# Hybrid decoder step on one core: VectorE's transposes and copies of a recurrence level put ahead of the serial steps of the pair before

## What is computed

```python
def rwkv_scan(S0, r, w, k, v, kk, a):
    def step(S, inp):
        r_t, w_t, k_t, v_t, kk_t, a_t = inp
        sa = jnp.einsum('bhvk,bhk->bhv', S, kk_t)
        S = S * w_t[:, :, None, :] - sa[..., None] * (kk_t * a_t)[:, :, None, :] + v_t[..., None] * k_t[:, :, None, :]
        y = jnp.einsum('bhvk,bhk->bhv', S, r_t)
        return S, y
    ...
    S, ys = lax.scan(step, S0, xs)
    return S, jnp.swapaxes(ys, 0, 1)
```

## Time and profile before

| | us |
|---|---|
| runs | 1202.17, 1209.87, 1207.2 (median 1207.2) |
| profiled execution | 1205.3 |
| its span, first to last instruction | 1203.5 |
| TensorE busy | 1119.9 (93%) |
| VectorE busy | 464.1 (39%) |
| ScalarE busy | 362.8 (30%) |
| GpSimd busy | 259.9 (22%) |

### The profile page before, as it was taken

One profiled execution on the slowest core, in us unless ns is written; L12 is line 12 of the kernel. 1 busy time (PEld: TensorE's weight loads), 2 busy tenths in 40 slices (PEclk: granted clock), 3 DMA queues, 4 the chain that ended last, 5 costly groups with the idle time before them and its releaser, 6 DMA issues.

```text
span 1203.5 us, 24875 instructions
## 1 busy us (share of the span) xinstructions
PE 1119.9 (93%) x10856; PEld 785.2 (65%) x10856; DVE 464.1 (39%) x930; ACT 362.8 (30%) x808; POOL 259.9 (22%) x153
## 2 busy tenths in 40 slices
PE   6999999999999878787789999989999999999995
PEld 4666666655566657666554444468878887888774
DVE  4200656356765675675744322350101001111024
ACT  4101645344334354564521221211111111011152
POOL 0000000001110169999800000111112112111102
PEclk9999999999999989999999999889999999999998
DMA  6511100010100220002032571169789989999894
GB/s 209 149 36 36 57 19 18 18 35 22 40 22 18 28 44 4 4 4 56 6 127 91 192 267 71 65 208 342 253 303 319 322 297 306 322 326 301 290 389 172
DMA packets 95689, 174.16 MB, mean 145 GB/s; under 512 B 19988, under 2 KB 41175, under 8 KB 95172
## 3 DMA queue, kind: packets, MB, share of 16 engines
q1 hardware_dynamic: 88372, 151.92, 36.5%
q0 software_dynamic: 7200, 20.57, 6.4%
HBM read 147.45 MB, written 27.75 MB: 146 GB/s over the span
## 4 chain that ended last, share of the span: by engine, by line
PE 84%; DVE 9%; ACT 3%; issue 3%; SPq 0%; DMA 0%; POOLq 0%; POOL 0%; DVEq 0%; ACTq 0%
PE ps L740 22%; PE ps L1446 20%; PE ps L1244 9%; PE ps L1469 9%; PE ps L1475 1%; PE ps L819 1%; PE ps L843 1%; PE ps L832 1%; PE ps L956 1%; PE ps L1422 1%; PE ps L944 1%; PE ps L997 1%; DVE ps L2283 1%; DVE arena L2272 1%; PE ps L986 1%
## 5 line engine op out<-in xcount | busy, mean ns | idle before, releaser
L740 PE MATMUL ps<-arena 128*128 128x355 f32 x960 | 298.7, 467 | 1.9 <-issue 1.8
L1446 PEld LDWEIGHTS ps<-arena 128*128 128x128 f32 x2048 | 245.9, 191 | 7.8 <-issue 6.1
L740 PEld LDWEIGHTS ps<-arena 128*128 128x128 f32 x960 | 180.2, 191 | 107.5 <-issue 10.5
L1446 PE MATMUL ps<-arena 128*128 128x128 f32 (+4 forms) x2048 | 248.3, 283 | 0.7 <-ACT arena L1958 0.6
L1244 PE MATMUL ps<-arena 128*128 128x512 f32 x256 | 116.4, 597 | 0.7 <-DVE arena L2346 0.7
L1469 PE MATMUL ps<-arena 128*128 128x512 f32 x256 | 113.3, 595 | 0.7 <-DVE arena L2621 0.7
L1966 ACT ACTIVATE arena<-ps 128x128 f32<-128x128 f32 (+4 forms) x64 | 18.3, 286 | 278.4 <-PE ps L1446 278.4
L2621 DVE TENSOR_TENSOR arena<-arena,ps 128x128 f32<-128x128 f32 (+4 forms) x64 | 19.1, 299 | 212.6 <-ACT arena L1966 212.6
L1469 PEld LDWEIGHTS ps<-arena 128*128 128x128 f32 x256 | 47.4, 190 | 55.1 <-issue 53.6
L2806 POOL TENSOR_TENSOR arena<-arena 128x1024 f32<-128x1024 f32 x4 | 11.4, 2855 | 331.5 <-DVE arena L2147 331.5
L1555 ACT COPY arena<-ps 128x355 f32<-128x355 f32 x60 | 27.2, 453 | 182.5 <-PE ps L740 182.5
(11 more groups left out here) (416 smaller groups left out, 1550.8 us busy)
## 6 DMA issues: line engine op xcount, KB each, us to landing
arena<-in_w_exp_gate SPq DMA_DIRECT2D x16, 2048.0 KB, 10.9
arena<-in_w_exp_up SPq DMA_DIRECT2D x16, 2048.0 KB, 16.0
arena<-in_w_exp_down SPq DMA_DIRECT2D x16, 2048.0 KB, 15.3
arena<-in_w_in SPq DMA_DIRECT2D x16, 512.0 KB, 3.8
arena<-in_x_prompt SPq DMA_DIRECT2D x9, 512.0 KB, 3.7
x_dram<-arena SPq DMA_DIRECT2D x9, 512.0 KB, 3.6
h_dram<-arena SPq DMA_DIRECT2D x8, 512.0 KB, 2.6
out_y_prompt<-arena SPq DMA_DIRECT2D x8, 512.0 KB, 3.5
```

What stands on the lines that cost most here:

```text
L740: last = pe.matmul(ps[:, q % 2, 0:m], wr[:, n % 3, k, :], hT[:, k, a:a + m], start=(k == 0), stop=(k == KB - 1))
L1446: last = pe.matmul(ps[:, 3 + f % 2, n * CAP:n * CAP + CAPS[e]], w[a][:, k, f * P:(f + 1) * P], xgT[:, a, k, 0:CAPS[e]], start=(k == 0), st ...
```

## The change

In the level loop of VectorE's stream, for every pair and level, the calls are written in another order. T1 of the level before stands ahead of `stepped(c)` instead of behind it; the copy of half 0 stands ahead of `stepped(c + 1)`; T0 and the copy of half 1 stand ahead of `stepped(c + 2)`. Nothing else differs.

```diff
--- before.py
+++ after.py
@@ -2405,20 +2405,20 @@
                 r_crossed(hp, 1)
                 for lv in range(1, LV):
                     c = 3 * (lv - 1) + 1
+                    r_transpose(hp, 1, lv - 1)
                     stepped(hp, c)
-                    r_transpose(hp, 1, lv - 1)
                     early_norm(hp, lv)
-                    stepped(hp, c + 1)
                     if lv < LV - 1:
                         r_x_in(hp, 0, lv)
                     else:
                         r_xt_in(hp, 0)
-                    stepped(hp, c + 2)
+                    stepped(hp, c + 1)
                     if lv < LV - 1:
                         r_transpose(hp, 0, lv)
                         r_x_in(hp, 1, lv)
                     else:
                         r_xt_in(hp, 1)
+                    stepped(hp, c + 2)
                     late_norm(hp, lv)
                 if hp >= 2:
                     g_scale(hp - 2, 1, 3)
```

## The result

The changed kernel takes 1197.83 us (median of 15 runs, 1191.21 to 1201.73), the kernel before 1206.09 in the 15 runs beside it (1200.81 to 1211.1). The ratio is 0.9929, 95% interval 0.9912 to 0.9945. By the ratio that is 8.6 us less, between 6.6 and 10.6; the two medians lie 8.3 apart. The profiled execution took 1199.22 us, its span 1197.4, against 1205.3 and 1203.5.

The account below looks back on a forecast made before the run. The last-ending chain is 84% TensorE, so time is won only where TensorE stands still. Terms: 0.8 + 2 x 3.0 = 6.8, less 1.1 for instruction stops, 5.7; 1207.2 - 5.7 = 1201.5 us, range 1195 to 1208.

Parts of the forecast that it names:

- (a): The forecast itself: in the levels, the copy of half 1 stops waiting needlessly; gain 3 to 9.5 us, chance 0.72.
- level 1, each of pairs 2, 3: T1 no longer stands behind `stepped(1)`, and the next T1 comes earlier: 1.25 us gained per pair.
- level 2, each: Pairs 2 and 3: earlier copy of half 1 shortens T1 to T1 from 5.09 to 4.46 us, gain 0.63.
- level 3, each: Pairs 2 and 3: T1 to T1 from 4.49 to 3.84 us, 0.65 on paper, 0.08 taken because of instruction stops.
- level 4, each: Pairs 2 and 3, where gate matmuls wait for `g_scale`: T1 to T1 from 6.47 to 5.73 us, gain 0.74.
- pair 1, to T1 of level 2: TensorE's fills hold the X matmuls as before, but T1 comes at 484.76 against 485.73: 0.97 us gained.
- level 5, each of pairs 2, 3: TensorE's first step waits for a later `stepped(c+2)`, delaying the U matmuls queued behind it: -0.3 us per pair.
- What is taken off it: Level 3 of pairs 2 and 3: TensorE may stop for instructions, so 2 x 0.57 = 1.1 us comes off.
- (b): Given back: instruction supply sets TensorE's pace, level gains return as stops in dense stretches behind; gain -1 to 2, chance 0.20.
- (c): Slower: late steps hold U matmuls of half 1, levels 2 to 5 lose 0.40 each; +4.8 us, chance 0.04.
- (d): Much faster: all idle time ahead of `stepped` inside the levels was on the path; 12 us or more, chance 0.04.
- The signs named: Profile after: L1074 wait well under 41.4 us, level 2 about 4.46, step 1.03 after T1, copy within 0.1, 4.41 unchanged.

Follow-up runs that it names:

- by-level kernel: Changed kernel, but with the old order, `stepped(c)` ahead of T1, in levels 2, 3 and 5 of pairs 2 and 3; 1196.66 us, ratio 0.9926.
- kernel with the fill behind: Changed kernel, with TensorE's late fill (L1122, L1136) behind half 1's X matmuls and the last step in levels 1, 2, 4 of pairs 2, 3; 1199.98 us.
- kernel with T1 first: Kernel before, with only T1 (transpose of half 1) moved ahead of `stepped(c)`; 1204.99 us, ratio 1.0003.
- kernel with half 1 first: Kernel before, with only T0 and the copy of half 1 moved ahead of `stepped(c + 2)`; 1201.85 us, ratio 0.9954.

## Why the prediction was right, and what was sized wrong

The forecast was 1201.5 us and "same", the measured median 1197.83, inside the range of 1195 to 1208 and within 1% of before. The mechanism is the one predicted, in the upper half of (a): 8.6 us won against 5.7. That no change under about 1% could be told from noise was too cautious; with 15 runs of each kernel the interval (0.9912 to 0.9945) excludes 1. Term by term, T1 to T1 (level 1 from T0 to T1), in us gained. The third column compares stretches at the same clock: for pairs 2 and 3 full clock in both kernels, for pair 1 the two first profiles, which both have a half-clock stretch in its level 1.

| term | predicted | measured at the same clock | mean of four profiles |
|---|---|---|---|
| level 1, each of pairs 2, 3 | 1.25 | 9.05 - 7.92 = 1.13 | 1.56, 1.45 |
| level 2, each | 0.63 | 5.09 - 4.47 = 0.62 | 0.62 |
| level 3, each | 0.65 on paper, 0.08 taken | 4.49 - 3.88 = 0.61 | 0.61 |
| level 4, each | 0.74 | 6.46 - 5.72 = 0.74 | 0.74, 1.29 |
| pair 1, to T1 of level 2 | 0.97 | 15.81 - 14.46 = 1.35 | 1.74 (to its last T1) |
| level 5, each of pairs 2, 3 | -0.3 | 4.22 - 4.39 = -0.17 to `g_scale` | |

**The step that failed** is "What is taken off it": 2 x 0.57 = 1.1 us for instruction stops in level 3. Level 3 went at 3.87 to 3.89 us in all eight cases, and at 3.56 in the by-level kernel, with no stop in it. That stops of 1.08 and 1.64 us stood in the dense stretch was no evidence about the levels, where TensorE still waits for others for part of each. In the changed kernel's four profiles, levels 1 to 4 of the three pairs show only two stops over 0.3 us (0.38 and 0.41), both in a level 4. The rule of the Trainium skill, page "Runtime: NRT & Kernel Launch", section "Instruction fetch mechanics", that the fetch is hidden, gave the better sum here (6.8). The traces don't bear it out as a general rule: the stop behind pair 2 was 1.57 to 3.76 us long in every kernel, with nothing to wait for. That these stops are instruction fetches is argued, by the prediction too; no view here shows it. The prediction had said that a level 3 at 3.84 would mean a gain nearer 6.8, and that is how it went.

**Too small: pair 1.** 0.93 of its 1.35 is the term predicted (T1 came 2.51 after the start of the X matmuls of level 2, and now comes 1.58 after it). The other 0.42 is that these X matmuls themselves came earlier, 12.88 after T0 instead of 13.30; the prediction had put this at nothing, "as before". They follow level 2's X matmuls of half 0 by 1.74 us instead of 2.23 (2.18 to 2.23 in the four profiles of before, 1.73 to 1.74 after), because the step between the two starts 0.47 after the first instead of 0.91. Ahead of that step TensorE stood for 0.21 to 0.27 us in every profile of before and not at all after; what it waited for, the profile doesn't show. Levels 3 and 4 were unchanged at 4.41, as predicted.

**Not in the sum at all: the clock in the levels.** Granted clock, kernel before, at pair 2's level 1, in the profile on which the prediction rests and in its third one (columns: window, its length, TensorE busy, granted clock, DMA share, GB/s). The first:

```profile
521.00:523.00 2.00, 0.69 (x32) 0.97 0.03 8
523.00:525.00 2.00, 1.96 (x53) 0.50 0.00 0
525.00:527.00 2.00, 2.00 (x65) 0.67 0.04 8
```

The same stretch in the third:

```profile
519.00:521.00 2.00, 1.83 (x82) 1.00 0.00 0
521.00:523.00 2.00, 1.76 (x38) 1.00 0.03 8
```

0.50 is the lower level, 1.2 GHz. In the first profile level 1 runs its first matmuls at it and takes 9.98 us; in the third it doesn't, and takes 9.05. The numbers of the earlier trace rows, on which the 1.25 rested, are from a half-clock stretch. The T1 worked out from them comes 8.73 after T0, and the changed kernel's half-clock level 1s in these pairs show 8.71 to 8.89; against full clock the gain is 1.13. In level 4 of pair 3 two of the four profiles of before lose another 1.1 us in this way (7.60 and 7.62 instead of 6.46), and none of the four of after does. This is from the timeline of before's third profile:

```profile
594.51 1.71 PE L1136 MATMUL ps<-arena,wgate 128*128 128x512 f32 x2 [0.65 <-DVE arena L2339]
596.15 1.13 PE L997 MATMUL ps<-arena 64*64 64x64 f32 x32
```

Averaged over four profiles the clock is worth 0.43 + 0.32 in level 1 and 0.55 in level 4. With 0.39 in pair 1, where the third profile of after alone ran level 1 at full clock, it makes 1.7 us, the difference between the 7.55 of the third column (1.35 + 2 x 3.10) and the 9.25 measured. The prediction had no such term, so this part of the gain was luck for it. That the change brings it isn't shown, and for level 1 it is unlikely: there the clock fell in 9 of 12 stretches before and in 6 of 12 after, 1.5 to 3.0 us after T0, while the first instruction that the change moves (T1) comes 3.44 after T0 or later. In level 4 the wait ahead of L1136 did get shorter (in pair 2 from 1.08 to 0.47), but four profiles of each kernel don't show that this keeps the clock up. What the mechanism itself gave is 7.55 less 2 x 0.17 for level 5, about 7.2 us, which lies inside the measured 6.6 to 10.6.

**The rivals.** (b) is refuted by the table of stretches and by the stops behind pair 2. (c) didn't occur: U of half 1 was ready in time, and only the 0.44 that each level's first step waits is left of it. In the kernel with the fill behind, this very thing happens (U of half 1 late), and there a level 2 takes 5.11. (d) is refuted: the wait ahead of `stepped` fell by 23.6 us and the time by 8.6; so most of it can't have been on the path.

**The signs named** held: L1074's wait 17.8 instead of 41.4; 4.47 for 4.46; the step 0.99 after T1 for 1.03; the copy 0.07 after the X matmuls; 4.41 in pair 1's levels 3 and 4.

**Open**: why a stop at the same place is 0 us in one execution and 2.9 in the next, and which executions lose the clock in a level; what the step in pair 1's level 2 waited for. The first two move single profiles by more than the change's terms.

## What to carry to other kernels

When a serial chain is laid between the stages of other work on an in-order engine, put its instruction behind whatever is already due, and then check that the chain, which gets later, still has work as cover at its own tightest place: here the third move wins about two thirds as much without the other two. Work such a change out with start-to-start times down the one queue that decides; that was right to 0.04 us for levels 2 to 4 (4.46, 3.84 and 5.73 worked out; 4.47, 3.88 and 5.72 measured). Before a stretch of one profile is used in a sum, look at its granted clock, and compare several profiles of each kernel before a difference in an untouched stretch is believed.

## What the hardware showed that was not expected

- TensorE's clock fell in some executions of one program and not in others, behind the same waits. In level 1 TensorE waits 0.48 and 1.16 us ahead of L966 and L974 in every profile of both kernels, and the clock fell there in 15 of 24 stretches. Ahead of level 4's gate matmuls (L1136) a wait of 0.65 us left it full in before's first profile and at half in its third; 1.21 in the kernel with T1 first left it at half, 1.25 in the kernel with half 1 first left it full. A fall there costs about 1.1 us (7.60 against 6.46).
- A stop of 1.92 us in the dense stretch behind pair 1 was followed by half clock in the profile after: 32 matmuls of L944 took 5.38 us, 3.71 in the profile before, 1.67 us more. The length of the stop doesn't decide it: behind one of 2.39 us L944 took 3.71 in before's first profile and 5.19 in after's second, behind one of 3.49 it took 3.71. The timeline of the first case:

```profile
506.15 0.27 PE L1058 MATMUL ps<-arena 64*64 64x64 f32 x1 [1.92 <-issue]
...
506.64 5.38 PE L944 MATMUL ps<-table,arena 128*128 128x128 f32 x32
```

The granted clock (fourth column) of the same stretch, where the profile before has 1.00 throughout:

```profile
504.00:508.00 4.00, 2.08 (x43) 0.91 0.00 0
508.00:512.00 4.00, 4.00 (x29) 0.67 0.02 4
```
